# Five slots of each second down projection by seven block products, and layer two's state-space preparation moved one feed-forward later

## The reference

```
for l in range(2):
    x = x + 0.5 * swiglu(rmsnorm(x), ffn1_w_in[l], ffn1_w_out[l])
    z = rmsnorm(x) @ mix_w_in[l]          # state-space group and gated group
    x = x + concat(rmsnorm(s5(z)), rmsnorm(gmlp(z))) @ mix_w_out[l]
    x = x + 0.5 * swiglu(rmsnorm(x), ffn2_w_in[l], ffn2_w_out[l])
return rmsnorm(x)
# swiglu(h, w_in, w_out) = (silu(g) * u) @ w_out,   g, u = halves of h @ w_in
```

## Time and profile before

| | |
|---|---|
| median of three runs | 914.44 us |
| span of the profiled execution | 913.7 us (0.7 us lie around it) |
| TensorE busy | 904.4 us, 99% |
| VectorE busy | 547.2 us, 60% |
| ScalarE busy | 482.5 us, 53% |
| GpSimd busy | 366.3 us, 40% |
| granted TensorE clock | 0.999 of full |

### The profile page before, as it was taken

One profiled execution on the slowest core, in us unless ns is written; L12 is line 12 of the kernel. 1 busy time (PEld: TensorE's weight loads), 2 busy tenths in 40 slices (PEclk: granted clock), 3 DMA queues, 4 the chain that ended last, 5 costly groups with the idle time before them and its releaser, 6 DMA issues.

```text
span 913.7 us, 12727 instructions
## 1 busy us (share of the span) xinstructions
PE 904.4 (99%) x4971; PEld 749.3 (82%) x4971; DVE 547.2 (60%) x617; ACT 482.5 (53%) x703; POOL 366.3 (40%) x571
## 2 busy tenths in 40 slices
PE   8999999999999999999999999999999999999997
PEld 6888888888878888888888888888888888888886
DVE  4655565458976555664485555544688855555544
ACT  6545454467766444444664444443577654545434
POOL 3488999893512688998850000000044100000000
PEclk9999999999999999999999999999999999999999
DMA  9786555544267756555455565556434466565551
GB/s 269 200 272 186 185 184 176 175 156 147 94 204 224 211 177 191 184 188 185 139 184 186 184 186 183 187 191 202 162 133 157 137 216 191 179 195 198 183 183 46
DMA packets 130123, 165.14 MB, mean 181 GB/s; under 512 B 18184, under 2 KB 109456, under 8 KB 130064
## 3 DMA queue, kind: packets, MB, share of 16 engines
q1 hardware_dynamic: 129776, 163.81, 56.4%
q10 hardware_dynamic: 288, 0.53, 0.2%
HBM read 163.27 MB, written 1.05 MB: 180 GB/s over the span
## 4 chain that ended last, share of the span: by engine, by line
PE 98%; DMA 1%; SPq 1%; ACT 0%; issue 0%; DVE 0%
PE bank L420 30%; PE bank L422 30%; PE bank L421 30%; PE bank L525 2%; PE bank L430 1%; PE bank L704 1%; DMA x<-in_x 1%; PE bank L732 0%; PE bank L722 0%; PE bank L745 0%; SPq L302 0%; PE bank L634 0%; PE bank L808 0%; PE bank L641 0%; PE bank L760 0%; PE bank L770 0%
## 5 line engine op out<-in xcount | busy, mean ns | idle before, releaser
L1150 DVE TENSOR_TENSOR w_lo<-raw,w_hi 128x1024 fp32r<-128x1024 f32 x302 | 382.2, 1271 | 300.5 <-ACT w_hi L870 300.3
L870 ACT ACTIVATE w_hi<-raw 128x1024 fp32r<-128x1024 f32 x302 | 318.7, 1062 | 304.0 <-PE bank L422 287.9
L420 PE MATMUL bank<-w_hi,x_hi 128*128 128x512 f32 x856 | 336.6, 393 | 0.0
L422 PE MATMUL bank<-w_hi,x_lo 128*128 128x512 f32 x856 | 333.4, 389 | 0.0
L421 PE MATMUL bank<-w_lo,x_hi 128*128 128x512 f32 x856 | 333.2, 389 | 0.0
L420 PEld LDWEIGHTS bank<-w_hi,x_hi 128*128 128x128 f32 x856 | 160.7, 188 | 35.3 <-issue 2.5
L422 PEld LDWEIGHTS bank<-w_hi,x_lo 128*128 128x128 f32 x856 | 160.7, 188 | 33.9
L421 PEld LDWEIGHTS bank<-w_lo,x_hi 128*128 128x128 f32 x856 | 160.8, 188 | 32.3
L1419 POOL TENSOR_TENSOR rstd_c<-ms_c,neg_half 128x2 f32<-128x2 f32 (+1 forms) x7 | 8.7, 1249 | 388.0 <-DVE ms_c L1170 388.0
L420 PE MATMUL bank<-w_hi,h_hi 128*128 128x512 f32 (+1 forms) x355 | 138.8, 391 | 0.0
L422 PE MATMUL bank<-w_hi,h_lo 128*128 128x512 f32 (+1 forms) x355 | 137.7, 388 | 0.0
(11 more groups left out here) (173 smaller groups left out, 597.3 us busy)
## 6 DMA issues: line engine op xcount, KB each, us to landing
raw<-in_ffn_w_in SPq DMA_DIRECT2D x172, 512.0 KB
raw<-in_ffn_w_out SPq DMA_DIRECT2D x44, 1024.0 KB
raw<-in_mix_w_in SPq DMA_DIRECT2D x12, 1024.0 KB
raw<-in_mix_w_out SPq DMA_DIRECT2D x8, 1024.0 KB
raw<-in_ffn_w_in SPq DMA_DIRECT2D x8, 256.0 KB, 5.0
gw<-in_ssm_glu_w SPq DMA_DIRECT2D x64, 2.0 KB, 2.8
x<-in_x SPq DMA_DIRECT2D x6, 128.0 KB, 5.4
out<-x SPq DMA_DIRECT2D x6, 128.0 KB, 2.1
```

The source lines that it names most:

```text
L420: mm(o, hi_a, hi_b, start=first, stop=False)
L422: return mm(o, lo_a, hi_b, start=False, stop=last)
L870: A(w_hi[:, n % RING, :], raw[:, s, (n % 2) * 1024:(n % 2) * 1024 + 1024], ACT.Copy).then_inc(hi_done, 1)
L1150: TT(w_lo[:, n % RING, :], raw[:, s, (n % 2) * 1024:(n % 2) * 1024 + 1024], w_hi[:, n % RING, :].bitcast(F32), ALU.subtract).then_inc(lo_d ...
```

## The change

Slots 4 to 8 (`SEVEN`, rows 1024 to 2303 of `ffn2_w_out`) of the second feed-forward of each layer are no longer two halves of four products each. A slot is a 2 x 2 block matrix (two blocks of rows by two of columns) against the 2 x 2 blocks of the hidden activations (two groups of tokens by two of rows). Winograd's form of Strassen's product gives the result with seven block products in place of eight, if sums of blocks are made first and the seven products are combined at the end. In the code:

- `seven_rows` (TensorE): 3 products of plain blocks, 9 matmuls, after the first `lo_done` of the slot, then 4 with summed or plain activations against summed weights, 12 matmuls, after the second. Four of the products go to four more banks.
- `seven_hi` (ACT): one copy of 1536 elements a partition (the three plain blocks), one of 2048 (the four sums). Before: two of 1024.
- `seven_lo` (DVE): the sums of the weights in three instructions (1024, 512 and 512 elements), of which the second waits for the first and the third for the second; a subtraction of 1536 and one of 2048. Before: two of 1024.
- the hidden activations of blocks 4 to 8: two small copies on ACT (`a21`), three sums on DVE (256, 128 and 128 elements), and one split of 512 more on each (`sums_hi`, `sums_lo`), at halves 37 to 41, 49 and 50.
- `first_product` (ACT) and `fold` (DVE): at half 65, ahead of the end of the stage, four banks are combined and added to x: one copy and eight instructions of 512 elements. All `residual`s of that stage, and the end of the kernel, wait for them.
- `load_seven` (SP): a slot comes in two transfers of 512 KB in place of one of 1 MB.
- the memory for this (`s_hi`, `s_lo`, `hs_lo`, `sums_b`, `a21`) lies where the tables of the preparation lie. So the preparation of layer two moves from the second feed-forward to the third, and POOL clears `gw`, `cw` and `kt_w` again before it, after the norm of the third feed-forward and after the last half of layer one.

The core of the diff:

```diff
@@ SP, load_ffn
-                        if p == 1 and b == 1 and kk == 0:
-                            sp.wait_ge(y_done, 2 * p)
-                            load_small(p)
+                        if j == 0 and b == 2 and kk == 0:
+                            if l == 0:
+                                load_gains()
+                            else:
+                                sp.wait_ge(half_done, half(l, 0))
+                            load_small(l)
...
+                    if j and k // 2 in SEVEN:
+                        load_seven(l, (DNS[j] + k) // 2, w_out, k)
@@ TensorE
+            def seven_rows(l, i, h, k, pairs, extra):
...
+                pe.wait_ge(lo_done, half(l, h) + 1)
+                product(p1[:, :], a11, *plain(B11), first, last)
+                product(c12[:, :], 4 + S4, *plain(B22), False, False)
+                product(c11[:, :], a12, *plain(B21), False, False).then_inc(half_done, 1)
+                pe.wait_ge(lo_done, half(l, h) + 2)
+                product(p5[:, :], 4 + S1, *summed(T1), first, last)
+                product(p7[:, :], 4 + S3, *summed(T3), first, last)
+                product(p6[:, :], 4 + S2, *summed(T2), first, last)
+                product(c21[:, :], a22, *summed(T4), False, False).then_inc(half_done, 1)
@@ ACT, seven_hi
+                if h % 2 == 0:
+                    act.wait_ge(raw_full[s], (n // 2 // RAW + 1) * 32)
+                    act.wait_ge(half_done, n - RING + 2)
+                    A(w_hi[...][:, 0:1536], raw[:, s, 512:2048], ACT.Copy).then_inc(hi_done, 1)
+                else:
+                    act.wait_ge(sb_done, 3 * m + 3)
...
+                    A(s_hi[:, m % 2, :], sums_b[:, m % 2, :], ACT.Copy).then_inc(hi_done, 1)
@@ DVE, seven_lo
+                if h % 2 == 0:
...
+                    TT(q[:, 0:2, :], b12.unsqueeze(1).broadcast_to([P, 2, 512]), plain[:, 0:2, :], ALU.subtract).then_inc(sb_done, 1)
+                    dve.wait_ge(sb_done, 3 * m + 1)
+                    TT(q[:, T2, :], plain[:, B22, :], q[:, T1, :], ALU.subtract).then_inc(sb_done, 1)
+                    dve.wait_ge(sb_done, 3 * m + 2)
+                    TT(q[:, T4, :], plain[:, B21, :], q[:, T2, :], ALU.subtract).then_inc(sb_done, 1)
+                    dve.wait_ge(hi_done, n + 1)
+                    TT(w_lo[...][:, 0:1536], raw[:, s, 512:2048], w_hi[...][:, 0:1536], ALU.subtract).then_inc(lo_done, 1)
+                else:
+                    dve.wait_ge(hi_done, n + 1)
+                    TT(s_lo[:, m % 2, :], sums_b[:, m % 2, :], s_hi[:, m % 2, :], ALU.subtract).then_inc(lo_done, 1)
@@ DVE, fold (at half 65 of the second feed-forward)
+                dve.wait_ge(p1_done, l + 1)
+                STT(u2, p6[:, :], 0.5, p1, ALU.mult, ALU.add).then_inc(fold_done, 1)
+                STT(xb[0][1], p5[:, :], 0.5, xb[0][1], ALU.mult, ALU.add).then_inc(fold_done, 1)
+                STT(xb[1][1], p5[:, :], 0.5, xb[1][1], ALU.mult, ALU.add).then_inc(fold_done, 1)
+                TT(xb[0][0], xb[0][0], p1, ALU.add).then_inc(fold_done, 1)
+                dve.wait_ge(fold_done, n + 4)
+                STT(u3, p7[:, :], -0.5, u2, ALU.mult, ALU.add).then_inc(fold_done, 1)
+                TT(xb[0][1], xb[0][1], u2, ALU.add).then_inc(fold_done, 1)
+                dve.wait_ge(fold_done, n + 5)
+                TT(xb[1][0], xb[1][0], u3, ALU.add).then_inc(fold_done, 1)
+                TT(xb[1][1], xb[1][1], u3, ALU.add).then_inc(fold_done, 1)
@@ POOL
             mix(0)
+            norm(norm_no(1, 0))
+            pool.wait_ge(half_done, half(1, 0))
+            clear_blocks()
+            prep_first(1)
             prep_rest(1)
             restart()
-            norm(norm_no(1, 0))
             mix(1)
```

More of the change, by code:

```diff
@@ L78, in half, with seven_of @@
     return l * HALVES + h
+def seven_of(h):
+    slot = (h - DN2) // 2
+    return SEVEN.index(slot) if h >= DN2 and slot in SEVEN else None
 def residuals(l, a):
@@ L645, in prep_groups, with product, plain, summed @@
                 ins.then_inc(prep_mm, 1)
+            def seven_rows(l, i, h, k, pairs, extra):
+                s, n = half(l, h) % RING, (l * N7 + i) % 2
+                a_hi, a_lo = [], []
+                for kk in range(2):
+                    for t in range(2):
+                        tok = slice(t * P, t * P + P)
+                        a_hi.append(h_hi[:, k + kk, tok])
+                        a_lo.append(h_lo[:, k + kk, tok])
+                a11, _, a12, a22 = range(4)
+                for q in range(4):
+                    a_hi.append(hs_hi[:, i, q * P:q * P + P])
+                    a_lo.append(hs_lo[:, i, q * P:q * P + P])
+                def product(o, a_, b_hi, b_lo, first, last):
+                    return three(o, a_hi[a_], a_lo[a_], b_hi, b_lo, first, last)
+                def plain(b):
+                    w = slice(b * 512, b * 512 + 512)
+                    return w_hi[:, s:s + 2, :].rearrange("p s m -> p (s m)")[:, w], w_lo[:, s:s + 2, :].rearrange("p s m -> p (s m)")[:, w]
+                def summed(b):
+                    w = slice(b * 512, b * 512 + 512)
+                    return s_hi[:, n, w], s_lo[:, n, w]
+                first, last = i == 0, i == N7 - 1
+                c11, c12, c21 = bank[2 * pairs[0]], bank[2 * pairs[1]], bank[2 * pairs[0] + 1]
+                p1, p5, p6, p7 = extra
+                pe.wait_ge(lo_done, half(l, h) + 1)
[7 more added lines that the diff above has]
+                product(c21[:, :], a22, *summed(T4), False, False).then_inc(half_done, 1)
             def ffn(l, j):
@@ L863, in split @@
                 s = (n // 2) % RAW
+                if seven_of(h) is not None:
+                    seven_hi(l, h, n, s)
+                    return
                 if n == 2:
@@ L1148, in split @@
                 s = (n // 2) % RAW
+                if seven_of(h) is not None:
+                    seven_lo(l, h, n, s)
+                    return
                 dve.wait_ge(hi_done, n + 1)
@@ L1640, in _, with clear_blocks @@
             link(nc.gpsimd.memset(neg_one[:, :], -1.0))
[L1641 to L1645, removed]
+            def clear_blocks():
+                link(nc.gpsimd.memset(gw[:].rearrange("p i f m -> p (i f m)"), 0.0))
+                pool.sem_inc(const_done, 1)
+                link(nc.gpsimd.memset(cw[:].rearrange("p a b c d e -> p (a b c d e)"), 0.0))
+                link(nc.gpsimd.memset(kt_w[:].rearrange("p a b c -> p (a b c)"), 0.0))
+            clear_blocks()
             restart()
```

202 lines of the change are left out of this document (145 added, 57 removed).

## The result

The changed kernel takes 923.65 us, the median of four runs (923.29 to 923.72). In the same session the kernel before took 914.38 (four runs). The ratio is 1.0103, 95% interval 1.0091 to 1.0114: slower by 9.3 us. The forecast was 922.3, slower.

A forecast was written before the change was run, and what follows sets the result against it. TensorE, busy 99% of the span, was taken to bound the kernel. Span 913.7 + 7.2 (DVE's pace) + 0.1 + 0.6 (the two layers' ends) = 921.6, plus 0.7 around it: 922.3 us; range 917 to 927.

The forecast's parts named there:

- DVE can't be hidden: Five slots a layer: DVE's chain takes 6.85 us a slot against TensorE's 4.76; each layer loses 3.6 us, two 7.2.
- the prediction's bounds: Period of the five slots: at least 6.25 us, at most 7.45, giving +1.1 and +6.0 us a layer.
- Rivals 1 and 2: Five slots: DVE keeps up, 908.3 us, chance 0.06; or no measurable change, period 5.9 to 6.1, 914 us, chance 0.04.
- Rival 3: Third feed-forward: POOL's preparation chain is late and the mixer waits some 3 to 5 us: 926 us, chance 0.07.
- Rival 4: Five slots: TensorE's idling lowers the clock to 1.2 GHz, ten slots take 41 us more: 955 us, chance 0.02.
- `load_seven`: Slot loads: two transfers where there was one, 1 MB as before; costs nothing.
- the sums of the activations: Halves 37 to 41, 49 and 50: some 1.9 us more DVE work in each of five blocks, nothing waits.
- the move: Layer two's preparation put into the third feed-forward: POOL's chain stays early enough, cost taken as 0.
- The end of the kernel: Layer two's end: `fold` and six DVE instructions finish 0.6 us late, on the path (0 to 2 us).
- the 0.1 for layer one's end: Layer one's end: `fold` delays the first `residual`, so TensorE gets x 0.1 us late.

The follow-up runs named there:

- the move alone: Changed kernel with no slot in the seven-product form and no `fold`, the preparation still moved: 914.87 us, ratio 1.0006 against the kernel before.

## Why the prediction was right, and where a size was off

**DVE can't be hidden.** Right. Period 6.86 against 6.85, by 1536 at 1.75 and 2048 at 2.29; a layer lost 3.60 and 3.58 where 3.6 was forecast. DVE began the slots 7.8 us ahead of TensorE (7.7 forecast), the five slots took 30.8 us (418.59 to 449.38, as forecast) and `fold` 5.0. The experiment with less work for DVE moved the period by 1.07, and the one that removed its waits left 6.46. Both point at the same limit. Two of the prediction's bounds have slips that nothing rests on: its own formula gives 1.2 and not 1.1 us a layer at a period of 6.25, and gaps of 0.10 throughout give 7.59 and not 7.45.

**Rivals 1 and 2** (DVE keeps up, or nearly) needed a period below 5.94, and of 5.9 to 6.1: out by the same rows. **Rival 3** is out by the move alone. **Rival 4** did not occur in this kernel: TensorE idles 1.3 us and 0.2 us in a slot's 6.86 and the granted clock reads 1.00 in both down projections. What the prediction cited beside this rival (the Trainium skill, TensorE: Matmul & The Clock Gate, section "A second HAM failure mode: psum-queue depth-cycling") is not borne out for such idles. But the rival was nearer than its 0.02 says: in the profiled execution of another kernel the clock fell behind a single wait of 1.99 us.

**`load_seven`, the sums of the activations, the move: nothing.** Right. TensorE's waits in the five slots are all for DVE's weights, and one slot costs the fixed price and no more.

**The end of the kernel: the term that was mis-sized.** 0.6 (0 to 2) was forecast and 2.07 measured, 1.47 more, which accounts for the miss of 1.35 us (the 0.1 for layer one's end did not show). Of the 2.07, 1.07 is `fold`'s lateness, for which 0.6 was forecast: the row of DVE instructions behind `fold` was worked out without the 0.28 us that DVE waits there for ACT's squares (912.34). The other 1.00 is a step that the prediction didn't have: a DVE instruction falls together with POOL's last multiplication. I gave L1570 the 0.74 that its forerunner L1378 took in the trace of before without looking at what ran beside it. There POOL's row, which is 1.27 long in both later kernels, took 1.73: this was the hint that the two get in each other's way.

**Span and median.** In all later runs 1.7 us lie around the span, not 0.7, so the profiled execution of before was about 1 us longer than the median one. It reaches the end of the first feed-forward at 199.09 us and that of after at 197.65, 1.4 earlier, though both kernels do nearly the same up to there. The two errors cancel in the forecast's sum, but a comparison of the two spans alone (913.7 and 921.6) would show 7.9 for a change of 9.3.

## What to carry to other kernels

Before trading TensorE's work for another engine's, divide that engine's elements per piece by TensorE's time per piece in the stretch itself: 5632 elements at 1.065 ns against 4.76 us decided this change, while the engine's 60% over the whole kernel said the opposite. The same form pays where it is thinned out until DVE keeps up: three slots with plain ones between them gave 0.2% (0.3% with POOL's multiplication moved as well) where five neighbours cost 1.0%. And ask of each moved instruction what now runs beside it and what stands behind it in its queue: one colliding instruction was worth 1.0 us, one block's split out of place 6.3.

## What the hardware showed that was not expected

- DVE and POOL in each other's way. A DVE instruction of 512 elements with two tensors in SBUF took 1.83 us when it started 0.01 us before POOL's 1.27 us multiplication of two tensors, and 0.75 alone. It ended 0.55 us after POOL's, 0.2 less than its time alone, so it can have begun only about when POOL was done. In the kernel before DVE was 0.16 us ahead, and POOL's took 1.73. The Trainium skill, SBUF — State Buffer, section "SBUF: two separate sides", says that the two share a pair of ports by an exclusive lock, held for a whole instruction by whichever starts first, which also binds a DVE instruction with two SBUF inputs when GpSimd's reads SBUF. The trace agrees that one of the two waits for the other. Who gets the pair can't be read from starts this close: in all eight kernels with this collision DVE's record starts 0.00 to 0.02 us ahead of POOL's, and it is DVE that waits.
- The granted clock fell to 0.50 behind a single wait of 1.99 us, 1.1 us after TensorE went on in layer one and 0.2 us after in layer two, for 3.4 us each time, in the profiled execution of one kernel, and never where waits were 1.3 us once in 6.86. Wait and fall together cost 3.7 us a layer: without them the second feed-forward went from 188.39 to 184.68. By the distances between matmuls some 2.1 of it is the wait and 1.6 the low clock. Whether every execution of that kernel had the fall stays open: its mean clock was 0.994 and 0.995 at 920.51, 919.87 and 919.42 us, but 0.997 at 918.92 and 916.99, which the kernel without the wait shows too.
- The bracket of a wait is not its cost: 0.2 cost 0.69 together with the small delays ahead of it, and 1.3 and 0.2 together cost 2.10.
